# Block two's queries, gates and output projection as tile pairs by seven products, with four orders of block one changed

## The reference

```python
def hybrid_layer(x, pos, norm_g, w_in, ...):
    h = rmsnorm(x, norm_g)
    proj = h @ w_in
    (a_q, a_k, a_v, a_f, a_z, b_cq, b_ckv, b_kr, b_z,
     c_q, c_k, c_v, c_z, gates) = jnp.split(proj, ...)
    y_a = causal_block_attention(a_q, a_k, a_v, FOX_DH ** -0.5, log_cum)
    y_b = causal_block_attention(q_b, k_b, v_b, ...)      # q_b, k_b, v_b from b_cq, b_ckv, b_kr
    y_c = sliding_window_sink_attention(rope(c_q), rope(c_k), c_v, sinks)
    branches = stack([y_a * silu(a_z), y_b * silu(b_z), y_c * silu(c_z)])
    proj_br = jnp.einsum('blnw,nwd->blnd', branches, w_branch)
    g = jax.nn.sigmoid(gates.reshape(B, L, 3, D_MODEL))
    merged = jnp.sum(g * proj_br, axis=2)
    return x + merged @ w_out                             # the residual
```

## Time and profile before

| | us |
|---|---|
| median of 3 runs | 4113.45 (4113.29 to 4117.14) |
| the profiled execution's own time | 4116.59 |
| its span, first to last instruction | 4114.8 |
| PE busy | 3953.5 (96%) |
| PE weight loads busy | 3181.8 (77%) |
| DVE busy | 1903.4 (46%) |
| ACT busy | 933.2 (23%) |
| POOL busy | 909.6 (22%) |

### The profile page before, as it was taken

The page is one execution under the profiler, slowest core; times in us unless marked ns, Lnnn a source line. Parts: engine busy times, 40 slices in busy tenths (PEclk is TensorE's granted clock), DMA queues, the critical chain, the costliest instruction groups (busy, mean ns, idle before and its releaser), DMA issues.

```text
span 4114.8 us, 68265 instructions
## 1 busy us (share of the span) xinstructions
PE 3953.5 (96%) x27684; PEld 3181.8 (77%) x27684; DVE 1903.4 (46%) x4410; ACT 933.2 (23%) x2376; POOL 909.6 (22%) x754
## 2 busy tenths in 40 slices
PE   8999989989999999989989999999999999999999
PEld 3667678878885676678878887878877788888877
DVE  5666665465413666665465413232334432223343
ACT  4233321112101223321112101232322112223220
POOL 0123325434431122314434442000110000011000
PEclk9999999999999999999999999999999999999999
DMA  3111102222222111102212222211112121121122
GB/s 127 32 37 42 41 17 83 92 62 92 83 91 77 37 42 47 32 17 95 87 62 87 88 87 68 61 52 57 57 52 61 58 67 57 52 62 57 60 59 67
DMA packets 70375, 257.90 MB, mean 63 GB/s; under 512 B 7808, under 2 KB 7936, under 8 KB 69808
## 3 DMA queue, kind: packets, MB, share of 16 engines
q1 hardware_dynamic: 68160, 246.42, 19.2%
q10 hardware_dynamic: 1904, 7.11, 0.5%
HBM read 249.31 MB, written 4.19 MB: 62 GB/s over the span
## 4 chain that ended last, share of the span: by engine, by line
PE 92%; DVE 5%; issue 1%; DVEq 1%; ACT 1%; ACTq 0%; DMA 0%; PEld 0%; PEldq 0%; SPq 0%
PE ps L2393 31%; PE ps L1505 27%; PE ps L2349 9%; PE ps L1524 2%; PE ps L1608 2%; PE ps L887 2%; PE ps L1668 2%; PE ps L843 2%; PE ps L2360 1%; PE ps L1627 1%; PE ps L2408 1%; PE ps L877 1%; PE ps L2422 1%; PE ps L1029 1%; PE ps L930 1%
## 5 line engine op out<-in xcount | busy, mean ns | idle before, releaser
L1505 PE MATMUL ps<-xT,ring 128*128 128x264 f32 (+2 forms) x3392 | 782.7, 386 | 0.0
L1505 PEld LDWEIGHTS ps<-xT,ring 128*128 128x128 f32 (+1 forms) x3392 | 632.9, 190 | 111.1 <-issue 10.8
L2393 PE MATMUL ps<-arena,ring 128*128 128x256 f32 x1856 | 433.1, 381 | 10.8 <-DVE arena L2730 5.5
L2393 PEld LDWEIGHTS ps<-arena,ring 128*128 128x128 f32 x1856 | 353.4, 191 | 60.5 <-DVE arena L2730 6.3
L2349 PE MATMUL ps<-xT,ring 128*128 128x512 f32 x864 | 385.6, 601 | 7.2 <-ACT xT L2556 6.3
L2393 PE MATMUL ps<-arena 128*128 128x256 f32 x1536 | 361.6, 380 | 0.0
L2349 PEld LDWEIGHTS ps<-xT,ring 128*128 128x128 f32 x864 | 163.0, 192 | 211.0 <-issue 209.9
L1505 PE MATMUL ps<-arena,ring 128*128 128x264 f32 (+1 forms) x1408 | 318.2, 384 | 6.0 <-DVE arena L1989 3.6
L2393 PEld LDWEIGHTS ps<-arena 128*128 128x128 f32 x1536 | 292.5, 190 | 40.0
L1505 PEld LDWEIGHTS ps<-arena,ring 128*128 128x128 f32 x1408 | 264.7, 190 | 50.7 <-DVE arena L1989 5.2
L2266 POOL TENSOR_TENSOR arena<-ring 128x512 f32<-128x512 f32 (+1 forms) x120 | 142.3, 1186 | 719.5 <-DMA ring<-in_weights 596.3
(11 more groups left out here) (385 smaller groups left out, 5922.9 us busy)
## 6 DMA issues: line engine op xcount, KB each, us to landing
ring<-in_weights SPq DMA_DIRECT2D x459, 512.0 KB, 3.6
arena<-skew_dram ACTq DMA_DIRECT2D x8, 448.0 KB, 3.2
arena<-in_x SPq DMA_DIRECT2D x1, 2048.0 KB, 8.1
out_rows<-arena SPq DMA_DIRECT2D x8, 256.0 KB, 3.3
skew_dram<-arena ACTq DMA_DIRECT2D x4, 511.5 KB, 7.0
consts<-in_const SPq DMA_DIRECT2D x1, 1256.0 KB, 10.7
consts<-in_const ACTq DMA_DIRECT2D x1, 1252.0 KB, 5.9
consts<-in_const SPq DMA_DIRECT2D x1, 128.0 KB, 2.5
```

The source lines that it names most:

```text
L1505: mm = pe.matmul(o[0:m, 0:cols.stop - cols.start], ws[:, k, 0:m], src[:, k, cols], start=k == 0, stop=k == nk - 1)
L2393: m = pe.matmul(bank_of(i, n), w[name][:, k, :], x[name](k), start=start and k == ks[0], stop=stop and k == ks[-1], skip_group_check=True)
```

## The change

Block two's tiles with the same input (queries of A and C with their `z`, all other `z` with a gate, gates with gates, `out` with `out`) are computed in pairs: 25 pairs a layer, each seven products of four matmuls in place of four halves of eight. A product is now the unit of the fill (`parts` 7, `cost` 1.83). POOL makes the weight sums of each pair in `sums2`, one buffer, four instructions of 512 columns, and the mixed inputs `tx2`, once a layer. `tx2` takes the place of `hT`, which is written to DRAM (`h_dram`) before and read back after the last gate; the mixes of `merged2` (`tm2`) take the place of `xT` at the tail. ACT copies product "1", DVE joins the other six in seven instructions (`join`; `add_out` for the residual); tanh runs once per pair afterwards, two units behind its last product. The output projection waits for `merged2` tile by tile. In block one four orders are changed.

```diff
-    return {"ms": 1, "mt": 1, "vb": 5, "uq": 6, "nc": 4, "cms": 4}.get(unit[0], 2)
+    return {"ms": 1, "mt": 1, "vb": 5, "uq": 6, "nc": 4, "cms": 4, "pair": 7}.get(unit[0], 2)
...
-    ("A", 3): [("uq", 0), ("z", "B", 0)] + [("g", 0, j) for j in range(2, 7)],
+    ("A", 3): [("uq", 0), two(("z", "B", 0), ("g", 0, 2)), gates(0, 3), gates(0, 5)],
...
+            def product(L, u, hf, o):
...
+                for k in range(4):
+                    if lead and name in "12":
+                        pe.wait_ge(*at("merged2", L, 2 * k + "12".index(name)))
...
+                    mm = pe.matmul(o[:, 0:n], w[:, k, :], x, start=k == 0, stop=k == 3)
...
+            def shape_two(L, u):
...
+                act.wait_ge(*at("two_made", SHAPED_AT[L, u]))
+                if u[1][0] == "g":
+                    j = u[1][2]
+                    m = act.activation(gb[:, j:j + 2, cols], gb[:, j:j + 2, cols], ACT.Tanh, scale=0.5)
...
+                if u == gates(2, 6):
+                    act.dma_start(hflat, h_dram).then_inc(h_back, 16)
...
+            def join(L, u, name, o, taken_):
...
+                dve.drain()
+                if name == "2":
+                    tt(a[:, c[0]], o, p1, ALU.add).then_inc(taken_, 1)
+                if name == "6":
+                    tt(p2, o, p1, ALU.add).then_inc(taken_, 1)
+                if name == "7":
+                    tt(p3, o, p2, ALU.add).then_inc(taken_, 1)
+                if name == "5":
+                    tt(p4, o, p2, ALU.add)
+                    tt(z[:, c[1]], o, p3, ALU.add).then_inc(taken_, 1)
...
+            def mix_x(L):
...
+                pool.wait_ge(h_stored, 16 * (L + 1))
+                pool.wait_ge(*at("hn", L, KD - 1))
+                tt(t1, b12, b11, ALU.subtract)
...
+            def weight_sums2(r):
...
+                if r:
+                    pool.wait_ge(*at("sums2_used", r - 1))
+                tt(s1, b1, b2, ALU.add)
+                pool.drain()
+                tt(s2, s1, a11, ALU.subtract)
+                pool.drain().then_inc(STEPS["sums2"][0], 2)
+                tt(b1, a11, b1, ALU.subtract)
+                pool.drain().then_inc(STEPS["sums2"][0], 1)
+                tt(s4, a12, s2, ALU.subtract)
...
             for s in range(NCH):
                 pnorm(s)
-                if c == GROUPS - 1:
-                    gate_mix(s)
                 if s < NCH - 1:
                     rowmax(s + 1)
...
                 if s == 3 and c < GROUPS - 1:
                     keys(dve, L, c + 1)
+                if c == GROUPS - 1:
+                    gate_mix(s)
...
-                        if jp == 0 and n == 2:
+                        if jp == 0 and n == 1:
                             took(dve, layA, a_pre(L), a_taken, f"oT@{GROUPS - 1}")
                             y_sums(L, 1)
...
-                seven(L, N_MRG, N_MRG, x, range(2), True, False, {"1": [at("merged_pair", L, 1)]})
-                seven(L, N_MRG, N_MRG, x, range(2, 4), False, True, {"1": [at("merged_pair", L, 3)]})
+                seven(L, N_MRG, N_MRG, x, range(3), True, False, {("1", 0): [at("merged_pair", L, 2)]})
+                seven(L, N_MRG, N_MRG, x, range(3, 4), False, True, {("1", 3): [at("merged_pair", L, 3)]})
...
-                    waits = {"1": [normed(L * 2 + 1, j) for j in range(4)], "2": [normed(L * 2 + 1, j) for j in range(4, 8)],
-                             "5": [at("tx", L, 0)], "6": [at("tx", L, 1)], "7": [at("tx", L, 2)], "4": [at("tx", L, 3)]}
+                    waits = {("12"[j // 4], j % 4): [normed(L * 2 + 1, j)] for j in range(KD)}
+                    waits.update({(nm, 0): [at("tx", L, m)] for m, nm in enumerate("5674")})
```

More of the change, by code:

```diff
@@ L150, in split @@
     def split(units):
-        return [(u, hf) for u in units for hf in range(parts(u))]
+        return [h for u in units for h in ([(u[1], hf) for hf in range(u[2], u[3])] if u[0] == "some" else
+                                           [(u, hf) for hf in range(parts(u))])]
     for L in range(LAYERS):
@@ L1751, in half @@
                 b = idx % 3
-                n = queries(L)[1] // 2 if kind in ("q", "z", "g", "br", "out") or (kind == "uq" and hf < 4) else HALF
+                n = queries(L)[1] // 2 if kind in ("q", "z", "br", "pair") or (kind == "uq" and hf < 4) else HALF
                 o = ps[:, FB[b], 0:n]
@@ L1761, in copy @@
                         m.then_inc(f_taken[b], 1)
-                if kind == "q" and u != ("q", "A", 0):
+                if idx in TANH_AT:
+                    shape_two(*TANH_AT[idx])
+                if kind == "pair" and hf == 0:
                     open_()
-                    copy(qk[:, pair_no(L, u[1], u[2]) % 2, 0, q_cols(L, hf)], o)
+                    copy(part2[:, 0, 0:n], o, scale=0.5 if u[1][0] == "out" else 1.0)
+                elif kind == "pair" and u[1][0] == "out" and hf == 6:
+                    for t in range(2):
+                        act.wait_ge(*taken(unit_at(L, *u[1 + t])))
+                        act.activation(sq2[:, u[1 + t][1], :], hT[:, u[1 + t][1], :], ACT.Square).then_inc(STEPS["sq2"][0], 1)
+                    if u[2][1] == KD - 1 and L < LAYERS - 1:
+                        act.drain()
+                        act.dma_start(h_dram, hflat).then_inc(h_stored, 16)
                 elif kind == "k" and u[1]:
@@ L1815, in half @@
                     copy(ncb[:, u[1] % 2, hf // 2, k_cols(hf % 2)], o)
-                elif kind == "g":
-                    open_()
-                    copy(gb[:, u[2], q_cols(L, hf)], o, True, ACT.Tanh, scale=0.5)
                 elif kind == "cms" and hf in (1, 3):
@@ L1936, in half @@
                 b = idx % 3
-                n = queries(L)[1] // 2 if kind in ("q", "z", "g", "br", "out", "sw") and u != ("sw", "k") else HALF
+                n = queries(L)[1] // 2 if kind in ("q", "z", "br", "pair", "sw") and u != ("sw", "k") else HALF
                 cols = q_cols(L, hf % 2) if n < HALF or L < LAYERS - 1 else k_cols(hf % 2)
@@ L1942, in open_ @@
                     dve.wait_ge(*made(idx))
-                if kind == "q" and u[1:] == ("A", 0):
+                if idx in ZS_AT:
+                    scale_z(*ZS_AT[idx])
+                if kind == "pair" and hf:
+                    if PRODUCTS[hf] == "2":
+                        dve.wait_ge(*taken(idx - 1))
+                    open_()
+                    (add_out if u[1][0] == "out" else join)(L, u, PRODUCTS[hf], o, f_taken[b])
+                elif kind == "q" and u[1:] == ("A", 0):
                     open_()
@@ L2507, in _ @@
                 var_parts(L * 2 + 2, BA[1])
[L2508 removed]
+            stack2_pe(pe, first, free, flush, done)
         @block.scalar
```

357 lines of the change are left out of this document (263 added, 94 removed), and 5 rows, old and new, of the table BESIDE.

## The result

| | before | changed |
|---|---|---|
| median of the runs | 4113.4 us | 3999.5 us (3993.1 to 4005.9, 4 runs) |
| ratio to before, 95% interval | | 0.9723 (0.9705 to 0.9740) |
| profiled execution: own time, span | 4116.6, 4114.8 | 3993.1, 3990.6 |

114 us less, against 99 forecast; 3999.5 lies in the range, on its better side. The profiled execution of the changed kernel was the quickest of its four, that of before lay 3 us above its median, so the two traces differ by 124 us, 10 more than the medians.

A forecast was written before the change was run, and what follows sets the result against it. Block two was taken to last as long as PE's matmuls. Terms -88.1 + 1 + 12 + 0 - 2.3 + 2.2 - 24 = -99 took 4116.6 to 4017.6; less 3.1 for the median, 4014.5 us, range 3990 to 4052.

The forecast's parts named there:

- The matmuls removed: Block two: 8 PE records fewer per pair, 25 pairs a layer, priced by record distance in unbroken runs: -88.1 us.
- Rival 5: Products: the saving is not real, PE's rate falling to that of its weight loads; no chance of its own given.
- The new breaks: Block two's fill: 216 places between attention's parts against 207, 0.1 to 0.2 us per new break: +1 us.
- DVE and POOL late: Block two: joins and POOL overlaps delay the scaling of probabilities, every third of 108 steps losing 0.35 us: +12 us.
- Rivals 1 and 2: Block two: DVE partly late in every step, 4057, chance 0.15; or attention chain becomes the bound, 4240, chance 0.04.
- Rival 2: Block two: scaling, transposes and exponentials wait on each other and become the bound, 238 us instead of 12: 4240, chance 0.04.
- The residual in DRAM: Around block two's layers: 2112 KB out and back, twice, 8 to 29 us each way, hidden behind other work: 0.
- Rival 4: Residual's transfers not hidden, a store taking 44 us, 15 us in each of two layers: 4044, chance 0.05.
- The tail: Kernel's end: wait before output projection goes, -2.3 us; wait before mean squares and the end each grow 1.1, +2.2.
- Block one: Four changed orders, each twice, shorten PE's waits and half-clock time: -24 us, bounds -12 and -30.
- 7.7, 8.5, 6.3 and 1.3: Block one, us gained by both layers: `gate_mix` later, `y_sums` earlier, output's first pass split later, feed-forward starting per tile.
- Rival 3: Block one gives nothing, its waits moving to DVE's next instruction: 4038, chance 0.08.

The follow-up runs named there:

- Experiment 3: The changed kernel with product 7 of every block-two pair given four more, overwritten matmuls, so as many records as before the change: 4089.5 us, +90.

## Why the prediction was right, and where not

The forecast rested on "block two lasts as long as its matmuls", and that held. By its steps:

- **The matmuls removed, -88.1.** Measured -87.7 of PE's busy time, and +90 when the eighth product was given back. Shown. Rival 5 (no real saving) is excluded by the same run. The forecast's sign for block two, 70 to 80 us shorter, was passed: 94.
- **The new breaks, +1.** Not seen: busy time with equal records differs by 0.5 us, in the other direction.
- **DVE and POOL late, +12. This is the term that failed.** PE's idle time in block two fell by 6.3; 2.3 of that was forecast elsewhere, and 0.4 came back at the tails: -4 in place of +12. These 16 us are about the whole of the 15 by which the median came out below the forecast. Two things were wrong. First, "every third step loses 0.35 us": a third of the steps do meet POOL at the scaling (34 of 108), but a meeting is seldom a loss. The prices under it were sound: a join takes 0.43 us, beside POOL too, and a scaling beside POOL takes longer. What was wrong is how many steps have no room: four waits for the scaling, 1.8 us together, where 36 steps were charged. The scaling's waits grew by 0.9 us, and with the gating (3.6) and one join (1.3) what was added comes to 5.8 us, not 12, although DVE got 214 us more to do and not the 150 that the forecast counted. The gaps of all steps would have said so (median 6.1 us before); I had measured one step with 5 us of room and argued from a constructed thinnest one. Second, the forecast had no term for the old waits that the finer units would shorten: those for L1989, L1970 and L1855 went from 10.5 to 1.4 us. Experiment 3 shows that the new order does this, not the missing matmuls; by which step of it was not tested.
- **Rivals 1 and 2** (late in every step) fell: even with DVE's joins doubled the cost was 9 us. Rival 2's mechanism exists: with POOL doubled PE waits for DVE and POOL, and 42 of the 111 us that would have turned the sign are lost.
- **The residual in DRAM, 0.** Right, with room: the copies landed in 6.8 and 9.2 us, at or below the short end of the 8 to 29 assumed, and no wait of PE names them. Rival 4 fell.

```profile
h_dram<-arena ACTq DMA_DIRECT2D x2, 2112.0 KB, 6.8
arena<-h_dram ACTq DMA_DIRECT2D x2, 2112.0 KB, 9.2
```

- **The tail, -2.3 and +2.2.** The wait ahead of the output projection is gone. The +2.2 did not come. Before, PE's last fill matmul ended at 4100.0, 14.8 us from the end; now at 3977.4 (3975.56 and 1.89), 13.2 from it:

```profile
3975.56 1.89 PE L1582 MATMUL ps<-xT,ring 128*128 128x256 f32 x8
...
3977.75 0.42 DVE L2189 SCALAR_TENSOR_TENSOR arena<-ps,arena 128x256 f32<-128x256 f32 x1
...
3979.46 1.05 PE L1790 MATMUL ps<-consts,arena 128*128 128x1 f32 x8 [2.01 <-DVEq L2009]
```

The wait grew from 1.8 to 2.0 only: DVE is done with product 3's tile at 3977.83, 0.4 us after PE ends product 4, so little of the second tile stands in the way (the forecast counted 1.1). The matmuls for the mean squares behind it took 1.05 and 1.06 us in place of 1.54 and 1.71: the clock fell 4.1 us after the last fill matmul, before 2.1 us after it.

- **Block one, -24.** The traces of seven executions with the new orders and three with the old give 2519.4 and 2544.8 us up to block two on average: -25; the medians, 20 to 25. Right in the sum, and at the edits' own places right in the parts too: 7.7, 8.5, 6.3 and 1.3 forecast, 9.1, 9.5, 5.8 and 1.4 found (table above). The extra 1 us for the clock at the output showed in the first pair of traces (2.9 and 4.8 in the two layers) and not in the experiment. In the two executions of the result `gate_mix` gains more, 6.0 and 4.7 us in the two layers, 10.7 in all. The clock is the likely reason. Behind a wait of 5.1 us it stood at 0.50 for eleven microseconds; behind one of 2.9:

```profile
560.00:564.00 4.00, 4.00 (x32) 4.00 (x32) 2.75 (x7) 0.68 (x2) 0.00 (x0) 0.83 0.02 4
564.00:568.00 4.00, 4.00 (x35) 3.50 (x35) 3.15 (x10) 1.84 (x7) 0.00 (x0) 1.00 0.01 2
568.00:572.00 4.00, 4.00 (x39) 4.00 (x38) 2.92 (x9) 1.60 (x6) 0.00 (x0) 1.00 0.00 0
```

(windows of the changed kernel as above: records of PE in brackets, the clock third from the end). It is back at 1.00 by 564, and PE gets through 35 to 39 records in 4 us, 20 or 21 in the kernel with `gate_mix` back. The forecast had losses of 1.5 and 5.5 us a layer for 3 and 11 us at half rate and charged 3.5 of the difference of 8 for both layers. Beyond the 4.4 us of shorter waits the clock gave 6.3 in this pair and 4.7 in the experiment, so the term was somewhat small, and this pair flatters it: this execution's 3.4 us at half rate are the shortest there; the other six with the same block one have 6.8 to 10.2 in the first layer.

Rival 3 (block one gives nothing) fell: 20 to 25.

## What to carry to other kernels

Where PE is busy 97% of a stretch, price a cut in matmuls by the distance between records in a long run, and take it whole; here it held within 2 us of 88. Before charging a lateness to every step, measure the room in all of them (end of the releasing instruction to the start of the waiting one): a mean or one step says nothing of the tail, and a constructed worst step is not the usual one. And price a wait of PE at what it does to the clock behind it as well, from the clock's record at that very place: a wait of 2.8 us cost 4.7 here, another of 2.7 cost 2.9. When small edits are priced singly, match the instructions at the edit's place; the medians were up to 5 us off.

## What the runs showed of the hardware

**DVE's tensor_scalar, tensor_tensor and scalar_tensor_tensor between SBUF tiles do not run slower beside POOL: they stand until POOL's current instruction ends.** The forecast took the 2.72 us of two scalings for DVE slowed down. The trace of the changed kernel has a case where no rate can be meant, two scalings of 16 by 16 elements (DVE and POOL in order of time):

```profile
3113.75 1.27 POOL L2386 TENSOR_TENSOR ring<-ring 128x512 f32<-128x512 f32 x1 [0.18 <-issue]
...
3113.89 1.30 DVE L2297 TENSOR_SCALAR arena<-arena 16x16 f32<-16x16 f32 x2
```

POOL's ends at 3115.02, and the first of the two scalings, by its own record, took 1.16 us, to 3115.05. An addition and a longer product in the mixer:

```profile
3092.61 1.31 POOL L2414 TENSOR_TENSOR arena<-arena,consts 128x528 f32<-128x528 f32 x1 [1.26 <-DVEq L2009]
3092.69 0.43 DVE L2123 SCALAR_TENSOR_TENSOR arena<-arena,ps 128x264 f32<-128x264 f32 x1 [0.21 <-issue]
...
3093.21 0.99 DVE L2125 TENSOR_TENSOR arena<-arena 128x264 f32<-128x264 f32 x1
...
3094.06 1.30 POOL L2416 TENSOR_TENSOR arena<-arena 128x528 f32<-128x528 f32 x1
3094.13 1.80 DVE L2136 SCALAR_TENSOR_TENSOR arena<-arena 128x528 f32<-128x528 f32 x1
```

L2123, which reads PSUM, passes beside POOL in its usual 0.43; L2125 (0.43 alone) and L2136 (0.70 alone) end 0.3 and 0.6 us behind POOL's instruction, a little less than their own time. Single lines, minimum, median and maximum in ns:

```profile
L2149 DVE TENSOR_TENSOR arena<-ps,arena x42: 423/428/433, 2584.1 to 3893.3; 128x264 f32<-128x264 f32 x21, 128x256 f32<-128x256 f32 x21
...
L2125 DVE TENSOR_TENSOR arena<-arena x64: 424/432/1443, 3051.2 to 3928.2; 128x264 f32<-128x264 f32 x32, 128x256 f32<-128x256 f32 x32
...
L2136 DVE SCALAR_TENSOR_TENSOR arena<-arena x22: 681/697/1807, 2595.3 to 3857.7; 128x528 f32<-128x528 f32 x11, 128x512 f32<-128x512 f32 x11
```

The joins (L2149 is one) never exceed 0.43; the others take up to 1.1 us more. The whole of block two says the same: 120 instructions of the three kinds with no tile in PSUM began while one of POOL's was running, and not one of them ended before it. Of the joins 31 began so, and 17 ended before POOL's did. Nor do all instructions between SBUF tiles stand: of 46 TENSOR_REDUCE and 24 RECIPROCAL that began so, 22 and 20 ended first. For the three kinds, then, one meeting costs DVE at most one instruction of POOL, some 1.3 us here, whatever DVE's own length. The Trainium skill, SBUF — State Buffer, SBUF: two separate sides, says just this: the shared pair of ports is an exclusive lock for a whole instruction and not a division of bandwidth, for GpSimd against a DVE instruction with two SBUF inputs or in a 2-port mode. The trace agrees, in the end of L2297 at the end of POOL's instruction. By it the 1.8 us that the forecast charged for an overlap are stays of two scalings, each of at most one POOL instruction, and no rate. Of the 216 scalings 65 overlap an instruction of POOL (17 before), and their sum rose from 84 to 104 us, of which PE saw 1.8.

**The same kernel's block one varies by the clock.** In seven executions with the same instructions in block one its length went from 2514.4 to 2522.8 us and the time at half clock in it from 38 to 55 us. The changed kernel itself was traced three times: 3990.6, 3994.5 and 3995.7 us, and all of that difference is block one's (2514.4, 2518.6, 2519.8; at half clock 38, 44 and 51 us). It sets what an edit of a few us can be told by.
